# Heads' loop written out, the attention outputs copied by two engines, and moved loads, joins and bias table in a single-core encoder layer

## The reference

```python
proj = x @ w_in[i]
aq, ak, av, ag, bq, bk, bv, bg = jnp.split(proj, split_at, axis=-1)
ya = chunk_relbias_attention(aq, ak, av, rel_bias[i])      # 8 heads, own chunk of 64 + 8 chunks before
ya = ya * jax.nn.silu(ag)
yb = sliding_window_sink_gqa(rope(bq), rope(bk), bv, sinks[i])   # 8 heads, own chunk + 1 before
yb = yb * jax.nn.silu(bg)
mix = jnp.concatenate([ya, yb], axis=-1) @ w_out[i]
h = DN_ALPHA * x + mix
h = h + jax.nn.sigmoid(h @ w_ple_gate[i]) * (p[i] @ w_ple_proj[i])
x = layer_norm(h, ln_g[i], ln_b[i])
```

## Time and profile before

| quantity | value |
|---|---|
| median of 3 runs | 2636.28 us (2633.91 to 2641.02) |
| profiled execution, its own time | 2638.49 us |
| its span, first to last instruction | 2636.6 us |
| PE busy | 2492.2 us, 95% of the span |
| DVE busy | 1715.5 us, 65% |
| ACT busy | 1180.6 us, 45% |
| POOL busy | 375.4 us, 14% |
| DMA | 402.60 MB, mean 153 GB/s |
| mean granted TensorE clock | 0.977 of full |

### The profile page before, as it was taken

One profiled execution on the slowest core, in us unless ns is written; L12 is line 12 of the kernel. 1 busy time (PEld: TensorE's weight loads), 2 busy tenths in 40 slices (PEclk: granted clock), 3 DMA queues, 4 the chain that ended last, 5 costly groups with the idle time before them and its releaser, 6 DMA issues. The chain is left out here.

```text
span 2636.6 us, 38499 instructions
## 1 busy us (share of the span) xinstructions
PE 2492.2 (95%) x13620; PEld 2166.1 (82%) x13620; DVE 1715.5 (65%) x3215; ACT 1180.6 (45%) x2406; POOL 375.4 (14%) x224
## 2 busy tenths in 40 slices
PE   6989999999999999999999998977999999999997
PEld 5778887888789878899999998866888888888886
DVE  8877787778786888378878786884333343433333
ACT  4343433343333434288878787862223222222322
POOL 0100000000000000000000000121444434344441
PEclk9989999999999999999999998988999999999999
DMA  3645265435544554656656547864435444444540
GB/s 132 197 143 161 103 204 160 135 126 189 163 123 151 183 161 107 215 186 213 207 168 194 165 126 255 290 183 145 122 109 128 115 122 118 111 121 108 126 117 25
DMA packets 353187, 402.60 MB, mean 153 GB/s; under 512 B 83576, under 2 KB 257800, under 8 KB 347272
## 3 DMA queue, kind: packets, MB, share of 16 engines
q1 hardware_dynamic: 349576, 391.39, 49.6%
q0 software_dynamic: 3456, 9.19, 1.1%
HBM read 265.50 MB, written 136.07 MB: 152 GB/s over the span
## 5 line engine op out<-in xcount | busy, mean ns | idle before, releaser
L1619 DVE TENSOR_TENSOR y_lo<-y_raw,y_hi 128x1024 fp32r<-128x1024 f32 x32 | 39.2, 1226 | 396.5 <-ACT y_hi L1127 396.5
L916 POOL DMA_DIRECT2D yb_d<-y_b x32 | 20.4, 636 | 1655.0 <-DVE y_b L1592 1655.0
L969 ACT ACTIVATE wop_hi<-w_raw 128x512 fp32r<-128x512 f32 x288 | 174.1, 622 | 181.7 <-DVE w_raw L1260 154.2
L1519 DVE CUSTOM_DVE_ANT_0 prob<-psum,bias 128x640 f32<-128x640 f32 (+4 forms) x256 | 199.3, 778 | 85.9 <-issue 85.5
L1098 ACT ACTIVATE prob<-prob,small 128x640 f32<-128x640 f32 (+4 forms) x256 | 204.0, 797 | 65.7 <-DVE small L1519 61.8
L1721 PE MATMUL psum<-wo_hi,y_hi 128*128 128x512 f32 x512 | 204.2, 399 | 7.5 <-DVE wo_lo L1614 7.5
L1721 PE MATMUL psum<-xs_lo_b,wop_hi 128*128 128x512 f32 x528 | 207.9, 394 | 0.0
L1721 PE MATMUL psum<-xt_hi,wop_hi 128*128 128x512 f32 x480 | 188.9, 393 | 17.6 <-DVE wop_lo L1265 7.2
L1535 DVE TENSOR_TENSOR pt_lo<-psum,pt_hi 128x640 fp32r<-128x640 f32 (+4 forms) x256 | 199.2, 778 | 6.7 <-ACT pt_hi L1107 6.6
L1721 PE MATMUL psum<-wo_lo,y_hi 128*128 128x512 f32 x512 | 201.4, 393 | 0.0
L1721 PE MATMUL psum<-wo_hi,y_lo 128*128 128x512 f32 x512 | 201.0, 393 | 0.0
(11 more groups left out here) (208 smaller groups left out, 6467.7 us busy)
## 6 DMA issues: line engine op xcount, KB each, us to landing
w_raw<-in_w_blocks SPq DMA_DIRECT2D x168, 256.0 KB, 4.0
qk_d<-stage_out SPq DMA_DIRECT2D x72, 512.0 KB, 3.9
v_d<-stage_out SPq DMA_DIRECT2D x64, 320.0 KB, 2.3
bq_d<-stage_out SPq DMA_DIRECT2D x64, 256.0 KB, 4.2
g_d<-stage_out SPq DMA_DIRECT2D x64, 256.0 KB, 2.3
ya_d<-y_a SPq DMA_DIRECT2D x128, 128.0 KB, 2.6
bq<-bq_d SPq DMA_DIRECT2D x32, 512.0 KB, 5.9
y_two<-ya_d SPq DMA_DIRECT2D x32, 512.0 KB, 4.7
```

The costliest lines, as they stand in the source:

```text
L916: pool.dma_start(yb_d[pair * P:pair * P + 4 * HEAD, t0:t0 + 4 * CHUNK].rearrange("(h d) t -> d h t", d=HEAD), y_b[:, d % 2, :, :]).then_in ...
L969: act.activation(wop_hi[:, n % W_RING, :, :], w_raw[:, i, :, :], ACT.Copy).then_inc(w_hi_done, 1)
L1519: dve.tensor_tensor_reduce(out=prob[:, r, NBW - n * P:NBW].rearrange("p (a b) -> p a b", a=2), in0=psum[:, 0:2, 0:n * P // 2], in1=bias[:, ...
L1619: dve.tensor_tensor(y_lo[:, :, :], y_raw[:, s, :, :], y_hi[:, :, :].bitcast(f32), ALU.subtract).then_inc(y_split, 1)
```

## The change

It has five parts. (1) The three later turns of the heads' loop are written out on ACT, DVE and PE. (2) The copy of a double's output is halved: ACT copies the first PSUM bank, DVE the second, each with its own semaphore; PE and POOL wait for both. (3) The copy of the bias table is issued by POOL, in two halves, as soon as the small table has been stored, and no longer by SP in the projection. (4) POOL's join of tile 0 comes one store later and waits for the last shift; that of tile 1 waits until the eight strips of `w_out` are split. (5) SP loads x of tile 1 and all of tile 2 but its p ahead of strips 16 and 17.

```diff
-                    if a == 4 and i == 0 and g == 0:
-                        sp.dma_start(bias_q_d.rearrange("(h q) c -> h q c", q=P), ...).then_inc(bias_stored, 16)
...
+            pool.wait_ge(setup_stored, 16 * 17)
+            for half in range(2):
+                pool.dma_start(bias_q_d.rearrange("(h q) c -> h q c", q=P)[:, half * 64:half * 64 + 64, :],
+                               ...).then_inc(bias_stored, 16)
...
             for t in range(2):
                 load_p(t, t)
+            sp.wait_ge(cw_split, KT - 1)
+            load_x(1, 1)
+            sp.wait_ge(y_joined, 1)
+            sp.wait_ge(y_ready, 1)
+            sp.wait_ge(y_split, 1)
+            load_tile(2, 0)
             for n in range(2 * KT, 2 * KT + 2):
                 sp.wait_ge(cw_split, n - 4)
                 load_strip(n)
-            load_x(1, 1)
...
-            next_tile(2, 0)
+            sp.wait_ge(p_split, 1)
+            load_p(2, 0)
...
             for d in range(B_DOUBLES):
                 store_yb(d)
-                if d == B_DOUBLES - 5:
+                if d == B_DOUBLES - 4:
+                    pool.wait_ge(bshift_ready, B_ALL)
                     y_tile(0, 0, True)
+            pool.wait_ge(cw_split, KT)
             y_tile(1, 1, True)
...
-            with act.Fori(1, A_HEADS // 2) as it:
+            for it in range(1, A_HEADS // 2):
                 for i in range(A_TURN):
                     a_step(it, i)
...
+                if step % 2 == 0 and 0 <= step - 8 and (step - 8) // 2 < B_DOUBLES:
+                    d = (step - 8) // 2
+                    act.wait_ge(bvalues_done, d + 1)
+                    if d >= 2:
+                        act.wait_ge(by_stored[d % 2], 16 * (d // 2))
+                    act.activation(y_b[:, d % 2, :, 0:2 * CHUNK]..., psum[0:HEAD, 4 + 2 * (d % 2), :]...,
+                                   ACT.Copy).then_inc(by_half_copied, 1)
...
-                    dve.tensor_copy(y_b[:, d % 2, :, :]..., psum[0:HEAD, 4 + 2 * (d % 2):6 + 2 * (d % 2), :]...
+                    dve.tensor_copy(y_b[:, d % 2, :, 2 * CHUNK:4 * CHUNK]..., psum[0:HEAD, 5 + 2 * (d % 2), :]...
```

More of the change, by code:

```diff
@@ L397, in build @@
         bvalues_done, by_copied = sem("bvalues_done"), sem("by_copied")
+        by_half_copied = sem("by_half_copied")
         by_stored = [sem(f"by_stored{i}") for i in range(2)]
@@ L641, in _ @@
                         sp.wait_ge(w_split, 72 * GROUPS)
-                        sp.wait_ge(bias_stored, 16)
+                        sp.wait_ge(bias_stored, 32)
                         load_bias(0, 0, first_loaded[0])
@@ L910, in _ @@
             pool.dma_start(bias_d[:, 0:384], bias_row[:, :]).then_inc(setup_stored, 16)
+            pool.wait_ge(setup_stored, 16 * 17)
+            for half in range(2):
+                pool.dma_start(bias_q_d.rearrange("(h q) c -> h q c", q=P)[:, half * 64:half * 64 + 64, :],
+                               bass.AP(tensor=bias_d.tensor, offset=127 - 64 * half, ap=[[384, A_HEADS], [-1, 64], [1, 256]])
+                               ).then_inc(bias_stored, 16)
             def store_yb(d):
@@ L915, in store_yb @@
                 pool.wait_ge(by_copied, d + 1)
+                pool.wait_ge(by_half_copied, d + 1)
                 pool.dma_start(yb_d[pair * P:pair * P + 4 * HEAD, t0:t0 + 4 * CHUNK].rearrange("(h d) t -> d h t", d=HEAD),
@@ L1163, in b_step @@
                                    ACT.Copy).then_inc(bprobsT_hi, 1)
+                if step % 2 == 0 and 0 <= step - 8 and (step - 8) // 2 < B_DOUBLES:
[3 more added lines that the diff above has]
+                        act.wait_ge(by_stored[d % 2], 16 * (d // 2))
+                    act.activation(y_b[:, d % 2, :, 0:2 * CHUNK].rearrange("p h (c q) -> p h c q", q=CHUNK),
+                                   psum[0:HEAD, 4 + 2 * (d % 2), :].rearrange("p (c h q) -> p h c q", h=4, q=CHUNK),
+                                   ACT.Copy).then_inc(by_half_copied, 1)
                 if step in (B_RECIP0 - 2, B_RECIP1 - 2):
@@ L1544, in _ @@
                 a_step(0, i)
-            with dve.Fori(1, A_HEADS // 2) as it:
+            for it in range(1, A_HEADS // 2):
                 for i in range(A_TURN):
@@ L1591, in b_step @@
                         dve.wait_ge(by_stored[d % 2], 16 * (d // 2))
-                    dve.tensor_copy(y_b[:, d % 2, :, :].rearrange("p h (c q) -> p h c q", q=CHUNK),
-                                    psum[0:HEAD, 4 + 2 * (d % 2):6 + 2 * (d % 2), :]
-                                    .rearrange("p a (c h q) -> p h (a c) q", h=4, q=CHUNK)).then_inc(by_copied, 1)
+                    dve.tensor_copy(y_b[:, d % 2, :, 2 * CHUNK:4 * CHUNK].rearrange("p h (c q) -> p h c q", q=CHUNK),
+                                    psum[0:HEAD, 5 + 2 * (d % 2), :].rearrange("p (c h q) -> p h c q", h=4, q=CHUNK)
+                                    ).then_inc(by_copied, 1)
                 u = step
@@ L1845, in _ @@
                 a_step(0, i)
-            with pe.Fori(1, A_HEADS // 2) as it:
+            for it in range(1, A_HEADS // 2):
                 for i in range(-1, A_TURN - 1):
@@ L1888, in b_values @@
                         pe.wait_ge(by_copied, d - 1)
+                        pe.wait_ge(by_half_copied, d - 1)
                     if i == 0:
```

3 lines of the change are left out of this document (removed).

## The result

The changed kernel takes 2607.7 us in the median (2606.84 to 2613.6) against 2637.41 us for the kernel before in the same series: ratio 0.9896, 95% interval 0.9881 to 0.9911. It is faster by 1.0%. The time lies inside the whole range forecast, 2588 to 2612 us, but above the 2588 to 2606 us of the case in which all five parts come near their values. Of the 39.5 us forecast 31.7 came: the profiled executions took 2638.49 and 2606.84 us.

A forecast was written before the change was run, and what follows sets the result against it. PE was taken to bound the heads' loop and nearly all of the output stage; gains of 13.0, 10.5, 2 and 14 us (parts 4 and 5 together) sum to 39.5 off 2638.49, forecast 2599 us, range 2588 to 2612.

The forecast's parts named there:

- the case in which all five parts come near their values: Whole kernel: the forecast case, time of 2588 to 2606 us, given 73%.
- The round: Middle of stage B: two units, from exponentials to exponentials, take 4.27 us instead of 4.75 with the copy halved.
- The slack of the stores: Stage B: a `y_b` buffer has about 7.5 us to be stored; median landing 5.5, at most 10.6; 3 us taken off.
- DVE's `y_lo` starts at 1765.0 instead of 1761.23: 3.8 us later, the price of this part: Entry to the output stage: tile 0's later join delays DVE's `y_lo` by 3.8 us.
- The sum: Entry, moved joins: chain from tile 0's join to its residual, starting at 1789.5 instead of 1792.55; gain 3 us.
- The wait of 11.57 us: Entry: PE's wait until 1831.31 for the residual of tile 1 goes with SP's new order, 11.6 us gained.
- strips 16 and 17 are now queued behind 2.3 MB of tile 2 [...] I put this at 1.5 us: Entry, before ple(0): the last two strips, which PE needs, come later through SP's new order; a loss of 1.5 us.
- the signs that I had named as making the forecast wrong: Changed profile: ACT and DVE waiting for the store in more than a few rounds, or PE waiting for `wp_lo`.
- the wait at the entry moves to the last strips: Rival at the entry: x and tile 2 delay strips 16 and 17 by 12 us, not 1.5; 2610 us; 8%.
- the 13 us by which tile 2 was issued earlier: Entry: SP issues x and tile 2 by about 1792, 13 us earlier, so tile 2's join is over near 1804.
- POOL's work and a DVE split do not run together: Entry, tile 1's join beside strip splits: times add; if both ran together the gain would be 6 us, not 3.
- the estimate of 9.4 us for a join and three splits: Entry: tile 1's join of 6.0 us plus splits of strips 8 to 10 at 1.14 each, 1780.1 to 1789.5.

The follow-up runs named there:

- no1: Changed kernel with the head loop of stage A as a loop again on PE, ACT and DVE: 2629.38 us, ratio 0.9968 to the kernel before.
- no2: Changed kernel with the whole output copy of a double on DVE again: 2625.16 us, ratio 0.9934 to the kernel before.
- drain_first: Changed kernel with the split of tile 0's y four steps later in ACT's and DVE's order: 2605.87 us, ratio 0.9885 to the kernel before.
- strips_only: Changed kernel with strips 16 and 17 issued between tile 2's first two loads and its reciprocals: 2603.83 us, ratio 0.9866 to the kernel before.
- tile1_late: Changed kernel with x of tile 0 and tile 1's loads held back until stage B's last shift: 2610.22 us, ratio 0.9881 to the kernel before.
- combined_plus: Changed kernel plus strips_only, drain_first, POOL's later LayerNorm wait, tile 0's `y_two` and `g_c` issued earlier, ACT's reciprocal copy ahead of tile 1's y split: 2601.4 us, 0.9864.
- tile0_late: Changed kernel with tile 0's own loads and x(0) held back until stage B's last shift: 2618.46 us, ratio 0.991 to the kernel before.

## Why the prediction was right or wrong

- **Part 1: right.** 13.0 forecast, 13.9 in the stretch, 14.9 by `no1`; no stretch of 64 steps is above 113.80 us.
- **Part 2: right, by its own steps.** 10.5 forecast, 11.7 in the stretch, 11.1 by `no2`. The round is 4.18 us where I took 4.27. ACT went from 79% to 98% busy, so that it now works nearly without a wait beside PE's 97%. The slack of the stores was right in the main: six of the 64 half copies waited for a store, 12.2 us in sum, and 10.8 of these are the two at 1723.75. That late store falls behind the last scores, so PE's 5.28 us there, 3.02 before, count in the next stretch and not in this one.
- **Part 3: right as far as it can be read**, 0.7 to 2.6 us in PE's waits against 2 forecast. Of the 5.4 us in the first row of the table most is luck.
- **Part 4: wrong, -0.6 us where 3 were forecast.** The step that failed is "DVE's `y_lo` starts at 1765.0 instead of 1761.23: 3.8 us later, the price of this part". Counted from the last scores it starts 18.3 us later instead of 11.4, 7.0 us more, 2.3 of them the late store's. I priced this as a delay of strips alone and overlooked what is queued behind `y_hi` and `y_lo` on both engines: the last transposes and values of stage B. PE's wait of 10.55 us there is new, where it had 2.56 and 3.58 before, and `drain_first` took part of it away. What the part was to do happened: the product of tile 0 is in one piece (1.16 us of wait instead of 5.82 and 1.65), and the residual of tile 0 starts 1.6 us earlier where 3 were forecast. The sum also ended one step too soon, at the residual: the transposes then wait 3.63 us for ACT's `recipb_t`, queued behind the split of tile 1, whose join is now later. From the residual to the transposes it is 3.59 us where it was 1.37, and this is 2.2 of the 3.6 us missing.
- **Part 5: wrong, 1.3 us where about 11 were forecast.** The wait of 11.57 us fell to 1.19, as said. The step that failed is "strips 16 and 17 are now queued behind 2.3 MB of tile 2 [...] I put this at 1.5 us". It was 7.79 us of wait, and after it ple and gate took 15.66 us, at a granted clock of 0.89 (1785.2 to 1802.2), where before they took 13.77 at 1.00 (1805.9 to 1820). PE's wait for the splits of these strips was among the signs that I had named as making the forecast wrong. From the last scores, ACT gets the first of the two strips 12.7 us later than before. `strips_only` shows the cause and how to have both: 57.3 us for the stretch, 8.0 less than before. This was the rival "the wait at the entry moves to the last strips", which I gave 8%; its price, 10.5 us more than forecast, was near.
- One wait stood in the code and I did not see it: POOL waits for the LayerNorm vectors ahead of its loop, and SP issues these only when all strips are split. The join of tile 2 stood 28.41 us for them and started at 1790.70, so that the 13 us by which tile 2 was issued earlier could not have come through whole. Here it cost little, 1.19 us at the transposes, as the strips held PE for longer; once they were out of the way it was the next wait, 3.33 us in `strips_only`.

So the sum was right in the two parts whose cycle had been measured in a steady state, and wrong in both where a chain of one-off waits was laid out by hand. That the time isn't at the very end of the range is luck: without the 3.4 us by which the projection came out better than forecast, the losses of 3.6 and 9.7 us would have made it some 2611 us. Most of the 3.4 us is scatter: kernels with the same projection code reached that mark between 1112.1 and 1119.2 us.

The step "POOL's work and a DVE split do not run together" was right, and the changed trace shows it instruction by instruction. DVE's timeline, the two of the 5.32 us taken apart:

```profile
1754.76 1.98 DVE L1633 TENSOR_TENSOR wg_lo<-strip_b,wg_hi 128x1024 fp32r<-128x1024 f32 x1 [0.25 <-ACT wg_hi L1196]
1756.66 3.41 DVE L1633 TENSOR_TENSOR wg_lo<-strip_b,wg_hi 128x1024 fp32r<-128x1024 f32 x1
```

The Trainium skill, "SBUF — State Buffer", summary rules, has a DVE instruction with two SBUF inputs and a GpSimd one that reads SBUF exclude each other: the second to issue waits until the first has finished. The trace agrees. POOL's product of 1755.63 takes 3.37 us where it takes 2.34 alone: it waits for DVE's split, which is over at about 1756.7. DVE's split of 1756.66 takes 3.41 instead of 1.22: it waits until that product is over, at 1759.0. POOL's next, of 1759.13, takes 3.15 and waits for DVE in turn. The two splits before the change took 8.05 us because all of the join, 6 us, fell between their start and their end; here only its middle did. So the estimate of 9.4 us for a join and three splits, in which all six stand in one row ahead of the residual, was too long: the last product went behind the third split, and the three splits were over 6.8 us after the start of the first.

**Open.** Which of tile 0's loads delays the stores. `tile1_late` rules out x(0) and tile 1, `combined_plus` rules out `y_two` and `g_c`; `r_c` and `y_raw` are left. The times of issue point to `r_c`: in `combined_plus` the late store was issued at 1708.40, behind both halves of `r_c` and ahead of `y_raw` at 1708.99, and in `tile0_late` at 1735.54, ahead of `y_raw` at 1736.30. But `y_raw` was under way beside them, and neither was tried by itself.

## What to carry to other kernels

When a wait is removed by moving loads forward in one queue, list all that the queue now issues later and by how much each of these may slip; here the place of two strips, ahead of the last three DMAs of a load or behind them, decided 6 us. When an engine is told to wait for a join, price what is queued behind it on every engine of the pipeline that is just draining, not only the work it is for. A steady round or a loop's turn could be priced to about 10% here from the distances of starts (13.0 for 13.9 and 10.5 for 11.7 us); the one-off chains at the border of two stages could not, so give such a chain the widest range, follow it to the next instruction of the engine that bounds, and make the edits there one at a time.

## What had not been expected of the hardware

- A turn of the loop costs 7.07 and 5.92 us (7.2 and 5.9 in `no1`) when three engines jump back; with the same code written out the distance is 113.80 us three times over, as short as without a jump before (113.61).
- A store of 256 KB lands in 3.0 us and, issued by POOL right behind the reciprocals `r_c` in SP's queue, in 12 to 13 us, while the core's DMA engines are busy for 72% of the time (1695 to 1728 us of the changed kernel).
- The same two strips of 512 KB, issued 1.3 us apart in two kernels, are 8 us apart in effect (1773.16 and 1781.30 on ACT): ahead of `r_c` and `y_raw` or behind them.
- While POOL's join runs, a strip's split on DVE of 1.2 us can take 4.88 us (`drain_first`), and a shift of 128x4 elements 3.19 us instead of 0.21.
